# Memory attention in a hybrid decoder step: prompt heads 0 to 2 move between the thirds of the query projection's tiles, head 3 and the single rows come behind it

## What is computed

```python
def cross_attn(h, mk, mv, w_cq, w_co):
    Bsz, L, _ = h.shape
    q = (h @ w_cq).reshape(Bsz, L, X_HEADS, X_HEADDIM)
    s = jnp.einsum('blhd,bmhd->bhlm', q, mk.astype(h.dtype)).astype(jnp.float32) * (X_HEADDIM ** -0.5)
    p = jax.nn.softmax(s, axis=-1).astype(h.dtype)
    o = jnp.einsum('bhlm,bmhd->blhd', p, mv.astype(h.dtype)).reshape(Bsz, L, D_MODEL)
    return o @ w_co
...
    x = x + cross_attn(rmsnorm(x, g_x), mk, mv, w_cq, w_co)
```

## Time and profile before

| what | value |
| --- | --- |
| median of 3 runs | 3430.09 us (3425.94 to 3430.66) |
| the profiled execution's own time | 3430.92 us |
| span of its trace | 3429.1 us |
| PE busy, share of the span | 96% |
| query projection on PE, attention, output projection's start | 2329 to 2421.6, to 2576.4, from there |

### The profile page before, as it was taken

One profiled execution on the slowest core, in us unless ns is written; L12 is line 12 of the kernel. 1 busy time (PEld: TensorE's weight loads), 2 busy tenths in 40 slices (PEclk: granted clock), 3 DMA queues, 4 the chain that ended last, 5 costly groups with the idle time before them and its releaser, 6 DMA issues.

```text
span 3429.1 us, 55043 instructions
## 1 busy us (share of the span) xinstructions
PE 3299.3 (96%) x21343; PEld 3171.1 (92%) x21343; DVE 1688.6 (49%) x2648; ACT 1014.2 (30%) x2224; POOL 980.8 (29%) x438
## 2 busy tenths in 40 slices
PE   8899999999999999999999798999899999999998
PEld 7899999998899999999999788999669999999998
DVE  5765566666300269988888734131342332223133
ACT  5344334444311144443444422121221211001010
POOL 3221222222122221222222002124343444445452
PEclk9999999999999999999999899999879999999999
DMA  4111111111222323322333463223241111111111
GB/s 136 46 51 45 35 34 44 50 44 44 94 75 79 90 58 95 93 75 71 95 90 82 119 216 131 73 88 104 81 147 37 50 43 45 48 49 43 49 43 68
DMA packets 340389, 253.81 MB, mean 74 GB/s; under 512 B 13788, under 2 KB 320549, under 8 KB 340197
## 3 DMA queue, kind: packets, MB, share of 16 engines
q1 hardware_dynamic: 324478, 232.55, 22.6%
q10 hardware_dynamic: 15792, 19.60, 1.6%
HBM read 205.76 MB, written 46.81 MB: 74 GB/s over the span
## 4 chain that ended last, share of the span: by engine, by line
PE 80%; DVE 11%; issue 4%; ACT 3%; DMA 1%; POOL 1%; DVEq 0%; SPq 0%; ACTq 0%; another core or an unknown queue 0%; POOLq 0%
PE psum L1049 9%; PE psum L1051 9%; PE psum L1050 9%; PE psum L1523 9%; PE psum L1525 9%; PE psum L1524 9%; PE psum L1183 4%; PE psum L1359 2%; PE psum L1361 2%; PE psum L1360 2%; PE psum L1319 1%; DVE arena L2291 1%; PE psum L1426 1%; PE psum L1174 1%; PE psum L1409 1%
## 5 line engine op out<-in xcount | busy, mean ns | idle before, releaser
L1049 PE MATMUL psum<-xh,whe 128*128 128x344 f32 x2304 | 777.8, 338 | 0.6 <-issue 0.6
L1050 PE MATMUL psum<-xl,whe 128*128 128x344 f32 x2304 | 740.9, 322 | 0.0
L1051 PE MATMUL psum<-xh,wle 128*128 128x344 f32 x2304 | 740.8, 322 | 0.0
L3099 POOL TENSOR_TENSOR wle<-slab,whe 128x1024 fp32r<-128x1024 f32 x104 | 267.9, 2576 | 1364.2 <-ACT whe L1700 1364.2
L1049 PEld LDWEIGHTS psum<-xh,whe 128*128 128x128 f32 x2304 | 438.3, 190 | 6.8 <-issue 2.3
L1050 PEld LDWEIGHTS psum<-xl,whe 128*128 128x128 f32 x2304 | 439.1, 191 | 0.6
L1051 PEld LDWEIGHTS psum<-xh,wle 128*128 128x128 f32 x2304 | 437.3, 190 | 0.0
L3191 POOL TENSOR_SCALAR wparts<-slab 128x1024 fp32r<-128x1024 f32 x80 | 221.8, 2773 | 505.7 <-POOLq L68 505.7
L1523 PE MATMUL psum<-at,wparts 128*128 128x344 f32 x960 | 308.0, 321 | 5.2 <-DVE r L3008 5.2
L1525 PE MATMUL psum<-at,wparts 128*128 128x344 f32 x960 | 306.7, 319 | 0.0
L1524 PE MATMUL psum<-xlow,wparts 128*128 128x344 f32 x960 | 306.2, 319 | 0.0
(11 more groups left out here) (417 smaller groups left out, 6509.9 us busy)
## 6 DMA issues: line engine op xcount, KB each, us to landing
slab<-in_w_in_dram SPq DMA_DIRECT2D x96, 512.0 KB, 3.9
arena<-d_rows SPq DMA_DIRECT2D x40, 512.0 KB, 5.5
slab<-in_w_ff_up_dram SPq DMA_DIRECT2D x32, 512.0 KB, 3.9
slab<-in_w_ff_down_dram SPq DMA_DIRECT2D x32, 512.0 KB, 3.6
out_dram<-arena SPq DMA_DIRECT2D x24, 512.0 KB, 4.5
arena<-in_state_ssm_dram SPq DMA_DIRECT2D x16, 512.0 KB, 6.0
d_yb<-arena SPq DMA_DIRECT2D x16, 512.0 KB, 4.5
slab<-in_w_ssm_up_dram SPq DMA_DIRECT2D x16, 512.0 KB, 3.6
```

What stands on the lines that cost most here:

```text
L1049: pe.matmul(out, w_hi, a_hi, start=(k == 0), stop=False)
L1050: pe.matmul(out, w_hi, a_lo, start=False, stop=False)
L1051: mm = pe.matmul(out, w_lo, a_hi, start=False, stop=(k == KT - 1))
L3099: pool.tensor_tensor(rounded(wle[slot]), slab[slot][:, :], whe[slot], ALU.subtract).then_inc(wlo_ready, 1)
```

## The change

Prompt heads 0 to 2 are put between the thirds of the query projection's tiles 2 to 7, by the table `CQ_AT`. Head 3 (and the last transposes and outputs of head 2) and the first single rows follow the projection by the list `AFTER_CQ`. The other single rows stand behind third 0 and third 1 of the output projection's first tile, by `CO_AT`; its third 2 holds the single rows' columns and comes after the last of them. To make room, the slots for the cached keys and values move into the buffer that holds the projection's low input part, so their first loads wait for the end of the projection and are issued by SP. The prompt's values and shares go to the buffer `xn`, which is free earlier. The outputs of heads 0 to 2 are written unrounded over the queries, and split into high and low in 128 x 1024 pieces behind the projection (`high_outputs`, `low_outputs`). The projection's tiles 2 to 7 are no longer a loop. The single rows' `os` is no longer interleaved.

```diff
-        kc, vc = ([xn[:, (2 * i + j) * MT * D:(2 * i + j + 1) * MT * D].rearrange("p (t c) -> p t c", t=MT)
+        kc, vc = ([dreg[:, (2 * i + j) * MT * D:(2 * i + j + 1) * MT * D].rearrange("p (t c) -> p t c", t=MT)
...
+        CQ_AT = {(2, 0): ["sc00"], (2, 1): ["sc01"], (3, 1): ["pt00"], (3, 2): ["o_00"],
+                 (4, 0): ["pt01", "sc10"], (4, 1): ["o_01", "sc11"], (5, 1): ["pt10"], (5, 2): ["o_10"],
+                 (6, 0): ["pt11", "sc20"], (6, 1): ["o_11", "sc21"], (7, 1): ["pt20"], (7, 2): ["o_20"]}
+        AFTER_CQ = ["pt21", "sc30", "o_21", "sc31", "pt30", "st00", "o_30", "pb00", "pt31", "st01", "os00", "o_31", "pb01",
+                    "st10", "os01", "pb10"]
+        CO_AT = {0: ["st11", "os10", "pb11"],
+                 1: ["st20", "os11", "pb20", "st21", "os20", "pb21", "st30", "os21", "pb30", "st31", "os30", "pb31", "os31"]}
...
@@ sync @@
+            sp.wait_ge(proj_full, 3 * W_CO)
+            for s in range(2):
+                cache_load("cache_mem_k", kc[s], kq_loaded[s], s)
...
             query_rows(0, 0)
             query_rows(0, 1)
+            for s in range(2):
+                cache_load("cache_mem_v", vc[s], vc_loaded[s], s)
...
@@ tensor @@
+            for j in range(2, KT, 2):
+                project3(j, W_CQ, lambda u, n, j=j: cq_before(j, u, n), xBv, xlow0,
+                         within=lambda u, n, j=j: cq_within(j, u, n))
+            query_transposes()
+            steps(AFTER_CQ)
...
+            project_all(W_CO, out_before, atv, atBv,
+                        within=lambda u, n: steps(CO_AT.get(n, ()) if u == 0 else ()))
...
@@ scalar @@
+            at_ = AFTER_CQ.index("pt30")
+            steps(AFTER_CQ[:at_])
+            high_outputs(range(2 * LAST - 2))
+            steps(AFTER_CQ[at_:at_ + 3])
+            high_outputs(range(2 * LAST - 2, 2 * LAST))
+            steps(AFTER_CQ[at_ + 3:])
...
@@ vector @@
+            largest(LAST, 0)
+            shares(LAST, 0)
             key_products(0, 0)
+            largest(LAST, 1)
+            shares(LAST, 1)
+            low_outputs(range(2 * LAST - 2), 0)
+            bias4(0, 0)
+            probs4(0, 0)
+            key_products(0, 1)
+            last_low(0, 2 * LAST - 2)
+            low_outputs(range(2 * LAST - 2, 2 * LAST), 2 * LAST)
+            bias4(0, 1)
+            probs4(0, 1)
+            key_products(1, 0)
+            out4(0, 0)
+            last_low(1, 2 * LAST + 2)
...
@@ gpsimd @@
+            for i in range(4):
+                split(W_CQ, 0, i)
+            lane.restart()
+            for n, (h, s) in enumerate(HALVES[:-2]):
+                normalise(h, s)
+                if n + 4 < KT:
+                    split(W_CQ, 0, n + 4)
+                lane.restart()
             key_products(0, 0)
+            normalise(LAST, 0)
+            normalise(LAST, 1)
+            for n, half_ in enumerate(HALVES[1:]):
+                if n < 2:
+                    split(W_CO, 0, n)
+                key_products(*half_)
```

More of the change, by code:

```diff
@@ L1571, in scores @@
-            def scores(h, s, beside=None):
-                def products(bk, i):
-                    for c in range(2):
-                        for k in range(2):
-                            yield pe.matmul(bk[:, c * M_N:(c + 1) * M_N],
-                                            qT[:, (2 * h + k) * NT + (4 * s + 2 * i + c) * P:][:, 0:P],
-                                            KTm[:, (2 * h + k) * M_N:(2 * h + k + 1) * M_N],
-                                            start=(k == 0), stop=(k == 1))
-                            done = 4 * i + 2 * c + k
-                            if beside and 0 < done < KT - 1:
-                                sample_out(*beside, done - 1, done)
-                for i in range(2):
-                    hand(G, f"sc{i}_{h}{s}", 0, lambda bk, i=i: products(bk, i))
-                if beside:
-                    sample_out(*beside, KT - 2, KT)
@@ L1589, in _, with cq_before, query_transposes @@
-            scores(0, 0)
-            scores(0, 1)
-            for m, (h, s) in enumerate(HALVES):
-                before = HALVES[m - 1] if m else None
+            def cq_before(j, u, n):
+                return (sum_taken, V_CO - 2 + n) if j + u == 0 else (proj_taken, 3 * j + (A_CQ + 3 * u + n - 2))
+            project3(0, W_CQ, lambda u, n: cq_before(0, u, n), xBv, xlow0, lambda k: (xl_ready, k + 1))
+            x_sums()
+            G = attn_plan
+            def query_transposes():
+                pe.wait_ge(q8s_ready, 1)
+                for j in range(2):
+                    hand(G, f"qt{j}", 0, lambda bk, j=j: (
+                        pe.transpose(bk[0:NB, i * P:(i + 1) * P], qT[:, (4 * j + i) * NT + T:(4 * j + i + 1) * NT],
+                                     ident[:, :]) for i in range(4)))
@@ new lines, in scores @@
+            def scores(h, s):
+                pe.wait_ge(proj_taken, A_CQ + 6 * h + 6)
+                for i in range(2):
+                    hand(G, f"sc{i}_{h}{s}", 0, lambda bk, i=i: (
+                        pe.matmul(bk[:, c * M_N:(c + 1) * M_N],
+                                  qT[:, (2 * h + k) * NT + (4 * s + 2 * i + c) * P:][:, 0:P],
+                                  KTm[:, (2 * h + k) * M_N:(2 * h + k + 1) * M_N], start=(k == 0), stop=(k == 1))
+                        for c in range(2) for k in range(2)))
@@ L1600, in _, with outputs @@
-                if h + 1 < XH_N:
-                    scores(h + 1, s, before)
+            def outputs(h, s):
                 taken(G, f"pt0_{h}{s}")
@@ new lines, in _, with steps, cq_within @@
+            STEP = {"sc": scores, "pt": share_transposes, "o_": outputs,
+                    "st": sample_scores, "pb": sample_shares, "os": sample_out}
+            def steps(units):
+                for unit in units:
+                    STEP[unit[:2]](int(unit[2]), int(unit[3]))
+            def cq_within(j, u, n):
+                if (j + u, n) == (2, 0):
+                    pe.wait_ge(xrn_ready, 1)
+                    hand(mem_plan, "xr8", 0, lambda bk: across(bk, lambda c: xrn[:, c:c + 1], [NC]))
+                steps(CQ_AT.get((j + u, n), ()))
@@ new lines, in last_low @@
+            def last_low(s, done):
+                for k in range(2):
+                    bk = got(G, f"o{k}_{LAST}{s}")
+                    dve.wait_ge(ohi_ready, done + k + 1)
+                    part_ = slice((2 * LAST + k) * NT + s * 512, (2 * LAST + k) * NT + s * 512 + 512)
+                    give(G, f"o{k}_{LAST}{s}", dve.tensor_tensor(rounded(atB[:, part_]), bk, at[:, part_], ALU.subtract))
+            for h, s in HALVES[:-2]:
+                largest(h, s)
+                shares(h, s)
@@ new lines, in _, with added @@
+            last_low(0, 2 * LAST - 2)
[6 more added lines that the diff above has]
+            lane.restart()
+            def added(k, wbase, thirds=range(3)):
+                for n in thirds:
+                    dve.wait_ge(proj_full, 3 * (wbase + k) + n + 1)
+                    dst = x1[:, k * NT + n * GW:k * NT + (n + 1) * GW]
+                    dve.tensor_tensor(dst, dst, psum[:, n, 0:GW], ALU.add).then_inc(sum_taken, 1)
@@ L2968, in _ @@
+            for n in range(2, len(HALVES)):
+                bias4(*HALVES[n])
+                probs4(*HALVES[n])
                 if n + 1 < len(HALVES):
                     key_products(*HALVES[n + 1])
[L2970 to L2975 removed]
+                out4(*HALVES[n - 1])
+                if n in (2, 3):
+                    added(0, W_CO, [n - 2])
```

209 lines of the change are left out of this document (87 added, 122 removed).

## The result

The changed kernel takes 3434.06 us (median of 20 runs, 3425.54 to 3438.17), the kernel before in the same runs 3427.08 (20 runs, 3416.15 to 3434.86). The ratio is 1.0021 with a 95% interval of 1.0013 to 1.0029, so 4.5 to 10 us slower, 7 in the middle: small, but clear of nothing by its interval. Forecast were 3431, a range of 3417 to 3441, and, as the likeliest case, no change that a measurement can tell (the prediction puts that limit at 7 us). The profiled execution of the changed kernel spans 3434.1 us, that of the kernel before 3429.1.

What follows compares the result with a forecast made beforehand. PE's waits of about 22 us and its lower clock were taken to bound the attention stretch. Terms 49.0 + 119.8 = 168.8 against 167.8 us gave 3431.9 profiled, 3431 median, range 3417 to 3441.

Steps and rivals of the forecast that it cites:

- the rival of the unhidden heads: In the projection, POOL's splits make PE wait 5.2 us at each of five transposes: 26 longer, 3457 us, chance 0.07.
- the sum of record lengths with 24 changes of instruction on top: In the projection, PE's pieces take 46.1 us, the rows' scale 0.3 and instruction changes 2.6: 49.0 us added.
- PE's wait for them: Behind the projection, PE stands from 15.9 to 23.9 us behind E until ACT's four copies are done: 8 us.
- ACT's last two copies let row 0's outputs start at 33.1: Behind the projection, row 0's outputs wait for these ACT copies and start 33.1 us behind E.
- The term for POOL: Normalising of (3,1) ends at 22.2 us behind E, a split at 27.4, then row 1's key products; scores ready at 31.6.
- DVE's multiply for row 0's shares held by POOL: POOL's key products may take the shared ports once more: 2.4 us, 1.2 reaching the end, 3433 for the profiled run.
- Loads set the pace: Behind row 2, loads of 9.36 us, key products 4.7, transpose 0.4 and outputs 6.7 make 21.2 us per two rows.
- The upper clock behind the projection: Faster rival: a row's outputs take 3.4 us and a third 3.8, 19.0 us less in all, 3412 us, chance 0.18.
- The lower clock: Slower rival: lower clock from 15.9 us behind E, PE's list the bound to row 4; 8.3 later, 3439 us, chance 0.20.
- decides once third 0 starts later than 57 behind E: Sign for the slower rival: the output projection's third 0 starting later than 57 us behind E.
- 46 of 68 us: Prompt work hidden under the projection, a gain spent again because eight rows then come in a row, nearly alone.
- its stretch at 0.50: In the kernel before, 2540 to 2576: rows' and prompt outputs alternate, clock 0.50, PE busy 35 of 36 us.

Runs made afterwards that it cites:

- keys_first: Changed kernel with SP asking for the keys of row n+3 ahead of the values of row n+2: 3425.09 us, ratio 1.0002 to the kernel before.
- split_later: Changed kernel with the key products of rows 1 and 2 ahead of the weight splits on POOL: 3425.31 us, ratio 0.9991 to the kernel before.
- two_orders: Changed kernel with both keys ahead of values on SP and key products ahead of weight splits on POOL: 3416.93 us, ratio 0.9981 to the kernel before.
- pe_filled: Changed kernel with unread 128 x 256 products put into PE's waits, in groups of 24, 28 and 16: 3445.63 us, ratio 1.0063 to the kernel before.
- pe_filled_half: Changed kernel with unread products in PE's waits, in groups of 12, 14 and 8: 3434.74 us, ratio 1.0018 to the kernel before.

## Why the prediction was nearly right

The time was in the range and the sum missed by little (42.6 and 128.1 make 170.7, forecast 168.8), but through two errors of opposite sign; that they nearly cancel is luck. The first row of the table takes the end of the projection from its first matmul: 135.0 us now, 92.4 before. The others count from E, the end of the projection (2465.66):

| event | forecast | measured |
|---|---|---|
| inserted work, E against the old end | 49.0 | 42.6 |
| row 0's key products done | 14.4 | 14.4 |
| ACT's four copies done | 22.7 | 22.0 |
| POOL: normalising of (3,1) done | 22.2 | 25.6 |
| row 1's scores ready | 31.6 | 35.5 |
| row 0's outputs start, end | 33.1, 38.1 | 38.4, 45.1 |
| third 0 added | 58.3 | 66.2 |
| row 2's outputs end | 63.0 | 69.9 |
| row 4's, row 6's end | 84.2, 105.4 | 91.0, 113.6 |
| third 2 added | 119.8 | 128.1 |

**Into the projection.** No idle, no wait for POOL, the upper clock: right, and the rival of the unhidden heads is out. The price was 6.4 too high. The step that failed is the sum of record lengths with 24 changes of instruction on top. Pieces follow each other 3.43 to 3.46 us apart where their records read 3.6 (2467.50, 2470.96, 2474.39), transposes 0.90 where they read 1.06. Sixteen pieces at these distances and the 0.3 for the rows' scale already make the 42.6, so no cost of the changes is seen.

**The head.** Right up to ACT's copies and PE's wait for them (6.2 instead of 8). Then the step "ACT's last two copies let row 0's outputs start at 33.1" failed: ahead of these outputs PE's list has the transposes of half (3,1), and their bank is freed by a subtraction on DVE that stands behind row 1's key products. Row 0 waited for row 1, which waited for POOL's split. The term for POOL was short as well, and that is the larger part: of the 5.3 us by which row 0 started late, row 1's scores bring 3.9 (35.5 for 31.6, with the normalising 3.4 late), and the subtraction and transposes behind them the rest. ACT's last two copies were done 31.3 behind E and held nobody up. The prediction weighed the port that the two engines share from one side only, POOL's two-input instruction holding DVE; here DVE's two-input subtractions held POOL's one-input normalising, 7.00 us for 3.62. The Trainium skill has that side too, page "SBUF — State Buffer", section "Who interferes with whom": a DVE instruction with two inputs in SBUF contends with a GpSimd instruction that reads SBUF. The runs agree, 7.00 beside the subtractions and 3.62 without them. The price that the prediction did weigh, DVE's multiply for row 0's shares held by POOL, was not paid: that multiply took 0.43.

**The rounds.** 21.2 forecast, 21.2 and 22.5 measured, and the lower clock was there (0.50). Of the 8.3 us by which the tail came late, all but 1.4 was there by row 2. "Loads set the pace" held, but with a cause that the prediction passed over: it took SP's order as given and priced the transfer, while keys_first hides the transfer by the order alone.

**The rivals.** The upper clock behind the projection did not come: 0.50. The lower clock "decides once third 0 starts later than 57 behind E"; it started at about 60, which the prediction also names as a sign of being wrong to the slow side, and the tail came out at that rival's 128.1. Yet PE's list at the lower clock is only part of it: between row 0's start and third 0's add it brought 2.6 us (27.8 for 25.2), while row 0 had started 5.3 late, and with PE's list untouched split_later starts row 0 5.7 us sooner and keys_first shortens the rounds by 7.5. That the rival's number came out is coincidence, and a condition can come true for another reason.

**The gain that went.** The prediction spoke of 46 of 68 us "gone under" and spent again. The runs without rows put it otherwise: there was hardly a gain to spend, 2 to 3 us, since PE pays for a prompt's piece wherever it stands while it is full. In their old place the pieces filled the rows' waits, and the rows now cost 9 to 10 us more. How much of that is lost cover, and how much comes from what else the change did to the rows (their outputs are no longer interleaved, their first loads start later), no run separates; the two orders alone bring back more than that.

## What to carry to other kernels

Work moved into a stretch where its engine is full is worth only the waits that it leaves behind; so measure first what the stretch costs without the other work that it covered. When cover is taken away, walk every in-order list once more, for each wait that stood at its head unseen: here a DMA queue's wait for one row held the next row's keys, and a weight split held a key product; two changes of order brought back 14 us. Size a probe from the trace before reading its outcome: products put into PE's waits to hold the clock up took longer than the waits, and so said little about the clock.

## What the runs showed of the hardware that was not expected

A list of one-column products keeps PE busy and at the lower clock all the same: 28.44 of 30 us busy at 0.61 in two_orders, and the wide form of the same sums 23.81 of 30 at 0.99. In two_orders the clock stands at 0.50 from 2528 to 2552 with PE busy all of these 24 us; the last wait before them is 1.56 us, and without a wait between the rows the level did not come back. The page of the Trainium skill that the prediction weighed ("TensorE: Matmul & The Clock Gate", section "HAM oscillation — how this bites in real kernels") tells of waits alone, and here the measurement goes further. The prediction let its stretch at 0.50 agree with that page, though PE was busy 35.15 of 36 us there.

The stretch of the kernel before took 160.4 and 167.8 us in two profiles of nearly the same instructions, at 0.82 and 0.77. Where the clock falls inside such a stretch is part of the spread of 3416 to 3437 us, and marks of one profile are good for no more than that. Another part lies far ahead of the change, in work that all these kernels share: the last third of the query is taken at 2462.42 in the profile of the changed kernel and at 2453.24 in that of keys_first, and from 1500 to 1540 the granted clock reads 0.87 in the one and 1.00 in the other. So the whole time of a single profile says little here.

A product of 128 x 256 in f32 leaves two records: 28 of them in pe_filled took 12.2 us at a clock of 1.00 (from 2488.94), so 0.44 us each; 24 took 12.21 at 0.86, and 12 took 6.45 at 0.82 in pe_filled_half.
